# The last probability product of the last attention unit, as two products of 64 output rows each

## What is computed

```python
for l in range(DEPTH):                       # 2 layers
    u = _rms_norm(x, pre_mix_norm_w[l])
    proj = u @ w_in[l]                       # all projections, the two gates among them
    y_a = gated_delta_rule(...) @ w_branch_a[l]
    # attention: 8 heads, 256 positions in two blocks of 128 queries
    p = softmax(masked scores)
    y_b = (p @ v_b) @ w_branch_b[l]
    h = gates[:, :, 0] * y_a + gates[:, :, 1] * y_b
    x = x + _rms_norm(h @ w_out[l], post_mix_norm_w[l])
    u = _rms_norm(x, pre_ffn_norm_w[l])
    f = jnp.square(jax.nn.relu(u @ w_ff1[l])) @ w_ff2[l]
    x = x + _rms_norm(f, post_ffn_norm_w[l])
```

## Time and profile before

| | |
|---|---|
| median of three runs | 1077.89 us (1075.48 to 1079.14) |
| span of the profiled execution, first to last instruction | 1064.2 us |
| median less that span | 13.7 us |
| TensorE busy with products | 1010.9 us (95% of the span), 10552 passes |
| VectorE / ScalarE / GpSimd busy | 732.4 / 557.7 / 137.9 us |
| mean granted TensorE clock (1 is 2.4 GHz) | 0.985 |

### The profile page before, as it was taken

The page is one execution under the profiler, slowest core; times in us unless marked ns, Lnnn a source line. Parts: engine busy times, 40 slices in busy tenths (PEclk is TensorE's granted clock), DMA queues, the critical chain, the costliest instruction groups (busy, mean ns, idle before and its releaser), DMA issues.

```text
span 1064.2 us, 24113 instructions
## 1 busy us (share of the span) xinstructions
PE 1010.9 (95%) x10552; PEld 987.3 (93%) x10552; DVE 732.4 (69%) x982; ACT 557.7 (52%) x786; POOL 137.9 (13%) x109
## 2 busy tenths in 40 slices
PE   5899899999999899999978999999999989999996
PEld 5899889899999899999978998998999979999995
DVE  6886648698566698745388766677875777886453
ACT  6576365755444554443356753767454445444441
POOL 6201000230000322200010000014000013221001
PEclk9999999999999899999989999999999999999998
DMA  7344424334556176666534443334356544766661
GB/s 252 135 141 158 124 82 130 118 106 149 188 180 197 65 224 192 200 196 195 160 119 135 143 142 121 115 106 121 117 166 189 166 153 145 213 197 199 193 185 40
DMA packets 45608, 163.85 MB, mean 154 GB/s; under 512 B 5184, under 2 KB 5440, under 8 KB 45504
## 3 DMA queue, kind: packets, MB, share of 16 engines
q1 hardware_dynamic: 44928, 161.50, 48.2%
q10 hardware_dynamic: 576, 0.82, 0.2%
HBM read 161.25 MB, written 1.05 MB: 153 GB/s over the span
## 4 chain that ended last, share of the span: by engine, by line
PE 91%; DVE 5%; issue 2%; ACT 2%; DMA 1%; POOL 0%; POOLq 0%; SPq 0%; ACTq 0%; DVEq 0%
PE dense L559 25%; PE dense L560 25%; PE dense L561 24%; DVE wlo L1296 1%; PE sides L945 1%; PE sides L799 1%; PE sides L919 1%; PE sides L920 1%; PE sides L791 1%; DVE utmp L1332 1%; PE sides L955 1%; PE sides L759 1%; PE sides L769 1%; PE sides L895 1%; PE sides L718 1%
## 5 line engine op out<-in xcount | busy, mean ns | idle before, releaser
L1296 DVE TENSOR_TENSOR wlo<-raw,whi 128x1024 fp32r<-128x1024 f32 (+1 forms) x304 | 397.9, 1318 | 195.8 <-ACT whi L973 195.5
L973 ACT ACTIVATE whi<-raw 128x1024 fp32r<-128x1024 f32 (+1 forms) x304 | 315.6, 1047 | 225.7 <-PE dense L561 222.0
L559 PE MATMUL dense<-uh,whi 128*128 128x256 f32 x768 | 223.3, 291 | 5.3 <-DVE wlo L1296 5.3
L560 PE MATMUL dense<-ul,whi 128*128 128x256 f32 x768 | 216.3, 282 | 2.6 <-issue 2.6
L561 PE MATMUL dense<-uh,wlo 128*128 128x256 f32 x768 | 216.3, 282 | 0.0
L559 PEld LDWEIGHTS dense<-uh,whi 128*128 128x128 f32 x768 | 147.2, 192 | 7.8 <-DVE wlo L1296 5.7
L559 PE MATMUL dense<-fuh,whi 128*128 128x256 f32 x512 | 144.3, 282 | 9.9 <-DVE ful L1632 9.6
L561 PEld LDWEIGHTS dense<-uh,wlo 128*128 128x128 f32 x768 | 147.2, 192 | 1.6 <-issue 1.6
L560 PEld LDWEIGHTS dense<-ul,whi 128*128 128x128 f32 x768 | 146.7, 191 | 1.5 <-issue 1.3
L560 PE MATMUL dense<-ful,whi 128*128 128x256 f32 x512 | 143.5, 280 | 0.0
L561 PE MATMUL dense<-fuh,wlo 128*128 128x256 f32 x512 | 143.5, 280 | 0.0
(11 more groups left out here) (289 smaller groups left out, 1923.2 us busy)
## 6 DMA issues: line engine op xcount, KB each, us to landing
raw<-weights SPq DMA_DIRECT2D x304, 512.0 KB, 3.7
xT<-x_t SPq DMA_DIRECT2D x4, 256.0 KB, 5.7
out_t<-xT SPq DMA_DIRECT2D x4, 256.0 KB, 2.3
cst<-consts ACTq DMA_DIRECT2D x1, 512.0 KB, 6.5
prm_all<-params ACTq DMA_DIRECT2D x1, 150.0 KB, 4.0
pos_i<-pos ACTq DMA_DIRECT2D x1, 128.0 KB, 5.5
cst<-consts ACTq DMA_DIRECT2D x1, 6.0 KB, 5.8
```

The source lines that it names most:

```text
L559: mm(o_, h_[:, ws], ahi[:, k0 + k, :], start=is_first, stop=False, skip_group_check=True)
L560: mm(o_, h_[:, ws], alo[:, k0 + k, :], start=False, stop=False, skip_group_check=True)
L973: return A(o_, i_, ACT.Copy)
L1296: TT(wlo[s][:, 0:w], raw[s][:, 0:w], f32(whi[s][:, 0:w]), ALU.subtract).then_inc(lo_ready, 1)
```

## The change

The last of the four products of `pv` 5 (head 7, kt = 1) is split by output rows: one product with value columns 0 to 63 into PSUM partitions 0 to 63, and one with columns 64 to 127 into partitions 64 to 127. Both add to what the product of kt = 0 left there. What is summed is the same.

```diff
                     for kt in range(qt + 1):
                         p_ = PT[n % 2][:, (e * (qt + 1) + kt) * P:(e * (qt + 1) + kt + 1) * P]
-                        r = mm(o_, vt[:, kt, h, :], p_, start=(kt == 0), stop=(kt == qt))
+                        if n == 5 and h == hs[-1] and kt == qt:
+                            for d in (slice(0, 64), slice(64, P)):
+                                r = mm(o_[d], vt[:, kt, h, d], p_, start=False, stop=True)
+                        else:
+                            r = mm(o_, vt[:, kt, h, :], p_, start=(kt == 0), stop=(kt == qt))
                 r.then_inc(pv_mm, 1)
```

## The result

The changed kernel takes 1063.82 us (median of 20 runs, 1055.97 to 1075.45), the kernel before in as many runs beside it 1073.54 us (1066.2 to 1082.18). The ratio is 0.9926, with an interval of 0.9905 to 0.9948: 0.74% faster. The forecast was 1073.7 us in a range of 1071.0 to 1077.8.

A forecast was written before the change was run, and what follows sets the result against it. The pace of dense products on TensorE was taken as the bound. Span 1064.2 - 5.2 gain + 1.0 cost = 1060.0 us, plus 13.7 us around it, gave 1073.7 us, range 1071.0 to 1077.8.

The forecast's parts named there:

- The bound: Whole kernel: TensorE is busy 95% of the span, so the pace of dense products or TensorE idling decides the time.
- the gain: `ya`, `yb` and `out`: 575 steps turn from 117.8 to 113.3 ns, saving 2.6 us per layer, 5.2 in two.
- The covers: Around `ya` to `out`: later `ah` and `al` hidden by over 21 us; `hl` ready for `out` with 1.2 us slack.
- The rule of the Trainium skill that was named as a rival: Dense products: step follows from moving width alone, 109 ns; only the cost stays, 1078.9 us; chance of neither layer quick 0.08.
- The cost: Split at `pv` 5: more passes, leaving and entering narrow products, 0.39 to 0.55 us per layer, taken as 0.5.
- the lower bound of 0.39: Split at `pv` 5: least cost per layer in us, with the second half running beside the first.
- the added passes: Split product of `pv` 5: four passes where two stood, 0.11 us if halves run side by side, 0.22 in line.
- entering and leaving: Around the narrow products of `pv` 5: 0.09 to 0.14 us to enter, about 0.19 us to leave.
- what settles the pace: Start of a dense stretch: narrow products right ahead mostly give the quick pace; quick in both layers had chance 0.75.
- 25 of 27: Earlier trace: places where dense products right behind narrow ones took the quick pace, used as a frequency.
- The base of the sum: Whole kernel: span 1064.2 us plus 13.7 us around it, matching the earlier median of 1077.89 us.
- The rival of the feed-forward part: Behind the wait for `wlo`: restart may come out slow, 6.4 us per layer, giving 1080.1 or 1086.5 us; chance 0.04.

The follow-up runs named there:

- full_dummy: Kernel before plus one plain full-size product (two passes, on constants) behind `pv` 5 in each layer: median 1061.95 us, ratio 0.9893 to before.
- twelve: Changed kernel plus one plain full-size product, ahead of `pv` 5 in layer 0 and behind it in layer 1: median 1071.1 us, ratio 0.9995 to before.

## Why the prediction was right and wrong

**The bound and the gain held.** The pace of dense products bounds the kernel, a stretch keeps its pace to its end, and the 1152 products concerned turned from 117.8 to 113.4 ns in all three traces of the changed kernel. 2.54 us per layer were measured and 2.6 forecast. The covers held as well: no idle time in the 65.40 us of `ya`, `yb` and `out`. The rule of the Trainium skill that was named as a rival (TensorE: Matmul & The Clock Gate, Back-to-back issue gap: 109 ns by the moving width alone) is given there for an isolated product, and does not describe these streams of weight loads and products: every long stretch has 113.3 to 113.4 or 117.8 ns at full granted clock.

**The cost was over-sized.** 0.5 us per layer was taken, 0.33 measured, below the lower bound of 0.39. The term that failed is that of the added passes, put at 0.11 us if the second half runs beside the first and 0.22 if all stand in line. The four narrow loads within 0.20 us show the halves side by side. With entering and leaving as they were taken from the earlier trace rows, 0.09 and 0.19 us, only 0.05 us is left for the passes, less than the one pass of the lower bound. The halves side by side agree with the Trainium skill, TensorEngine Tiling (Array Packing), Key Properties, that different tiles may run in parallel.

**The step "what settles the pace" was wrong, and gave the right answer.** The prediction saw 25 of 27 quick stretches behind narrow products and used this as a frequency; the same places of the changed kernel have 18 of 27. full_dummy turns the pace with nothing narrow, and twelve stays slow with narrow passes in the last place. At this place the pace goes with the number of passes, ten quick and twelve slow, and the split happened to add one pair: that `ya` turned quick was luck. With one plain product more the same split leaves `ya` slow (twelve), where the prediction would have forecast a quick one. How this comes about inside TensorE is not shown by any run, nor whether it is the number or a time that repeats. It is no rule for other places either: twelve passes turn the pace between `gate` 5 and 6 and leave it slow ahead of `ya`, and behind the wait of the feed-forward part narrow passes turned five slow pieces of six and no quick one.

**The base of the sum was wrong, and with it the range.** "With the 13.7 us around it" set a profiled span of 1064.2 us against a median of three runs. Around the span lie 1.8 us (1066.51 - 1064.7). The profiled execution of before was one with both feed-forward stretches quick, about 1066.0 us, and the three runs were on the slow side: 20 runs have a median of 1073.54, that is 4.35 us lower. The range took this median as "known to about 1 us"; the 20 runs have a standard deviation of 4.4 us, which makes a median of three uncertain by some 3 us (an estimate, 1.25 x 4.4 over the root of 3). The forecast of 4.2 us below 1073.54 would have been 1069.3, and the measured median lies 5.5 us lower still. The 4.4 us of the traces in place of 4.2 explain 0.2 of these. Over all the runs above the two means are 7.0 us apart and not the 9.7 of these medians, so some 2.7 us are the luck of these twenty runs each, and 2.6 stay open.

**The rival of the feed-forward part was misjudged.** It had a chance of 0.04, because "both layers passed it well" in a single trace. Its mechanism and its price were right (6.4 us forecast, 6.28 measured, at the place of the earlier trace rows). But it need not come from the change: the pace behind that wait falls anew in each execution, 13 of 36 slow, in kernels with slow and with quick `ya` alike. Such a stretch in the profiled execution hides the gain in the span, 1064.7 after 1064.2.

**What stays open.** The runs gained 7.0 ± 0.7 us, the traces explain 4.4. Setting the pace of the feed-forward part gained 4.2 us on the kernel before (1071.64 to 1067.48), and only 0.9 ± 0.7 on the changed one (1064.68 to 1063.77). With that pace set, what the change gains is the 3.7 ± 0.6 us above, which the traces explain. That would fit feed-forward stretches that are slow less often in the changed kernel. The traces lean this way, 7 of 14 against 6 of 18, and are too few to show it. So the remaining 2.6 us have no cause that was shown.

## What to carry to other kernels

Divide the length of each long stretch of same-shaped products by their count: two paces for one shape mean time that no wait shows, and one plain product ahead of the stretch, 0.22 us here, can be worth 2.5 us. Set one in, look at the trace of several executions, and try one pair of passes more or less before you believe a reason. Don't set a single profile's span against a median of other runs: first learn which of the kernel's paces that execution had.

## What the hardware showed that was not expected

- Two steady paces for one shape at full granted clock, 113.3 to 113.4 and 117.8 ns a product, held over as many as 1415 products without a wait, with 174 to 197 GB/s of DMA beside them.
- Ahead of `ya` the pace repeats in every trace and turns with each added pair of passes (8, 9, 12 and 16 slow, 10 and 14 quick); elsewhere twelve passes in the same 1.45 us turn it. Behind a wait of TensorE for VectorE it falls either way, in repeats of one program too: 13 of 36 slow, 6.28 us for 1415 products.
- One product of 128 output rows in two halves of 64 costs 0.33 us in all, and the four narrow weight loads take 0.20 us together; the next weight load starts after 0.17 us of idle time.
